# Squared-relu stages of a two-block transformer: four more output tiles as seven block products, and border squares in other buffers

## The reference, cut to what matters

```python
h2 = rms_norm_2(x, norm2) * (1.0 + scale2) + shift2
ff = jnp.square(jax.nn.relu(h2 @ w_ff1)) @ w_ff2
x = x + gate2 * ff
```

## Time and profile before

| | |
|---|---|
| runs | 3072.89, 3073.14, 3079.54 us; median 3073.14 |
| profiled execution | 3072.16 us, span 3070.4 us |
| PE busy | 3035.4 us, 99% of the span |
| DVE, ACT, POOL busy | 61%, 38%, 22% |
| granted PE clock, mean | 0.997 |
| part 3 in REL_1 | up(3, 2) to up(3, 7) 2990.54 to 3023.20 us, down(3, 0) to down(3, 7) 3023.20 to 3067 us |
| part 3 in REL_0 | 2430.94 to 2463.61 us, and 2463.61 to 2507.19 us |

### The profile page before, as it was taken

One profiled execution on the slowest core, in us unless ns is written; L12 is line 12 of the kernel. 1 busy time (PEld: TensorE's weight loads), 2 busy tenths in 40 slices (PEclk: granted clock), 3 DMA queues, 4 the chain that ended last, 5 costly groups with the idle time before them and its releaser, 6 DMA issues.

```text
span 3070.4 us, 39047 instructions
## 1 busy us (share of the span) xinstructions
PE 3035.4 (99%) x15394; PEld 2499.0 (81%) x15394; DVE 1884.7 (61%) x2899; ACT 1168.8 (38%) x1877; POOL 670.0 (22%) x525
## 2 busy tenths in 40 slices
PE   9999999999999999999999999999999999999999
PEld 7888887788888888887778888776799977779997
DVE  6454557554555445536774455677777856877775
ACT  4322334333223322234443222446544334654442
POOL 2101134111011110044311100346211123721111
PEclk9999999999999999999999999999999999999999
DMA  5343432243443434431133344310333232033232
GB/s 191 117 154 123 127 98 73 86 140 118 155 130 115 137 117 154 134 108 62 35 127 117 120 155 134 115 37 21 107 103 110 98 110 67 20 95 110 97 102 77
DMA packets 115814, 329.86 MB, mean 107 GB/s; under 512 B 13616, under 2 KB 19120, under 8 KB 115248
## 3 DMA queue, kind: packets, MB, share of 16 engines
q1 hardware_dynamic: 115632, 327.36, 33.2%
HBM read 325.21 MB, written 2.10 MB: 107 GB/s over the span
## 4 chain that ended last, share of the span: by engine, by line
PE 92%; DVE 4%; ACT 2%; POOL 1%; issue 1%; DMA 0%; SPq 0%; DVEq 0%; ACTq 0%; POOLq 0%
PE ps L83 91%; PE ps L86 1%; ACT s_tmp L89 1%; POOL s_tmp L100 1%; DVE s_wl L92 1%; DVE s_tmp L92 1%; DVE s_tmp L112 0%; DVE s_x L95 0%; ACT s_wh L89 0%; DVE s_small L106 0%; DVE s_tmp L100 0%; POOL s_tmp L92 0%; DVE s_tmpr L92 0%; ACT s_hh L89 0%; DMA s_raw<-in_f1i_dram 0%
## 5 line engine op out<-in xcount | busy, mean ns | idle before, releaser
L83 PE MATMUL ps<-s_hh,s_wh 128*128 128x512 f32 x2304 | 894.6, 393 | 20.2 <-ACT s_hh L89 11.6
L89 ACT ACTIVATE s_wh<-s_raw 128x1024 fp32r<-128x1024 f32 (+3 forms) x560 | 530.6, 951 | 951.9 <-PE ps L83 949.7
L83 PE MATMUL ps<-s_hh,s_wl 128*128 128x512 f32 x2304 | 888.2, 391 | 0.2
L83 PE MATMUL ps<-s_hl,s_wh 128*128 128x512 f32 x2304 | 887.3, 390 | 0.0
L92 DVE TENSOR_TENSOR s_wl<-s_raw,s_wh 128x1024 fp32r<-128x1024 f32 (+3 forms) x529 | 595.9, 1127 | 428.1 <-ACT s_wh L89 427.5
L92 POOL TENSOR_TENSOR s_tmp<-s_tmp 128x512 f32<-128x512 f32 (+2 forms) x228 | 306.8, 1350 | 1692.6 <-ACT s_tmp L89 1531.7
L83 PEld LDWEIGHTS ps<-s_hh,s_wh 128*128 128x128 f32 x2304 | 433.3, 188 | 117.6 <-issue 16.8
L83 PEld LDWEIGHTS ps<-s_hh,s_wl 128*128 128x128 f32 x2304 | 433.9, 188 | 93.2 <-DVE s_wl L92 2.5
L83 PEld LDWEIGHTS ps<-s_hl,s_wh 128*128 128x128 f32 x2304 | 434.1, 188 | 90.9 <-issue 2.2
L83 PE MATMUL ps<-s_a0h,s_wh 128*128 128x512 f32 (+1 forms) x1024 | 381.8, 373 | 0.0
L83 PE MATMUL ps<-s_a0h,s_wl 128*128 128x512 f32 (+1 forms) x1024 | 378.4, 370 | 0.0
(11 more groups left out here) (167 smaller groups left out, 3618.7 us busy)
## 6 DMA issues: line engine op xcount, KB each, us to landing
s_raw<-in_ff_dram SPq DMA_DIRECT2D x128, 512.0 KB, 3.7
s_tmp<-in_w_mod_dram SPq DMA_DIRECT2D x192, 256.0 KB, 3.6
s_raw<-in_f1i_dram SPq DMA_DIRECT2D x88, 512.0 KB, 3.6
s_raw<-in_f2i_dram SPq DMA_DIRECT2D x88, 512.0 KB, 3.6
s_raw<-in_f1o_dram SPq DMA_DIRECT2D x32, 512.0 KB, 3.5
s_raw<-in_f2o_dram SPq DMA_DIRECT2D x32, 512.0 KB, 3.6
s_raw<-in_hyb_dram SPq DMA_DIRECT2D x28, 512.0 KB, 3.5
s_raw<-in_nsa_dram SPq DMA_DIRECT2D x28, 512.0 KB, 3.6
```

Of the source, the lines that this page charges most:

```text
L83: return self.eng.matmul(o, w, m, **kw) if self.eng is not None else Blank()
L89: return self.eng.activation(o, a, f, **kw) if self.eng is not None else Blank()
```

## The change

In part 3 the output tiles 2 to 5 are now made by two groups, (3, 2) and (3, 4), and tiles 0, 1, 6 and 7 stay plain. So the differences, `a1h` and `a1l` are made in part 3 too, and weight sums for two more pairs. The sums are placed anew: `sum` 0 and 6 follow group(2, 6), `sum` 2 stands before group(3, 4) and `sum` 4 behind it; the buffers of PAIRS are exchanged to fit. The squares of x at the border from REL_0 to NSA_1 go to buffers 8 to 15 (which hold `hl`), as 38 to 42 are now in use by weight sums. The list of steps now ends: group(2, 6), sum 0, sum 6, up(3, 2), load, evac(3, 0), evac(3, 1), up(3, 3), load, evac(3, 2), up(3, 4), load, evac(3, 3), up(3, 5), load, evac(3, 4), up(3, 6), load, evac(3, 5), up(3, 7), load, evac(3, 6), sums, down(3, 0), evac(3, 7), load, down(3, 1), add(3, 0), load, tile 0, add(3, 1), tile 1, group(3, 2), sum 2, tile 2, tile 3, group(3, 4), sum 4, tile 4, tile 5, down(3, 6), load, down(3, 7), add(3, 6), load, tile 6, add(3, 7), tile 7.

```diff
--- before.py
+++ after.py
@@ -23,7 +23,7 @@
 FIRST_BANK = {F1_0: 4, F2_0: 0, F1_1: 4, F2_1: 0}
 GATE_BANK = (1, 0, 0, 1)
 UP_TILE = (0, 4, 1, 5, 2, 6, 3, 7)
-EARLY = (3, 2, 2)
+EARLY = (3, 2, 2, 0)
 UP_BANK = ((0, 1, 2, 3, 4, 0, 1, 2), (7, 6, 5, 0, 1, 2, 3, 4), (7, 6, 0, 1, 2, 3, 4, 5), (7, 6, 0, 1, 2, 3, 4, 5))
 LATER, SOONER = slice(T // 2, T), slice(0, T // 2)
 
@@ -467,7 +467,7 @@
     def down(p):
         for d in range(0, KT, 2):
             us = [stream.add(w2[d + m, :, p * 1024:(p + 1) * 1024], 1024) for m in range(2)]
-            if p == 3:
+            if p == 3 and d in (0, 6):
                 order.extend((("down", p, d + m), [us[m]]) for m in range(2))
             else:
                 stream.group(us)
@@ -494,9 +494,16 @@
         elif kind == "down":
             steps.append(("down", p, i, us[0]))
         else:
+            if added:
+                steps.extend([("add",) + added, ("tile", added[1])])
+                added = None
+            if p == 3 and i == 4:
+                steps.extend([("sum", 2), ("tile", 2), ("tile", 3)])
             steps.append(("group", p, i, us[0]))
             if p == 2 and i == KT - 2:
-                steps.extend([("sum", 4), ("sum", 6)])
+                steps.extend([("sum", 0), ("sum", 6)])
+            if p == 3 and i == 4:
+                steps.extend([("sum", 4), ("tile", 4), ("tile", 5)])
         if added:
             steps.append(("add",) + added)
         if kind != "group":
@@ -512,8 +519,6 @@
                 steps.append(("load", n))
             if n + 1 in stream.second and n - 1 not in stream.second:
                 steps.append(("sums", n + 1))
-            if (kind, p) == ("up", 3) and i in (3, 5):
-                steps.append(("sum", i - 3))
         if added:
             steps.append(("tile", added[1]))
             added = None
@@ -710,8 +715,8 @@
         def two(ap):
             return ap.rearrange("p (a c) -> p a c", a=2)
 
-        PAIRS = {0: (two(S(36)), two(S(37))), 2: (two(ssum2[:, :]), two(rstd[:, :])),
-                 4: (mix_tmp[:, 0:2, SOONER], mix_tmp[:, 8:10, SOONER]), 6: (mix_tmp[:, 2:4, SOONER], mix_tmp[:, 10:12, SOONER])}
+        PAIRS = {2: (two(S(36)), two(S(37))), 4: (two(ssum2[:, :]), two(rstd[:, :])),
+                 0: (mix_tmp[:, 0:2, SOONER], mix_tmp[:, 8:10, SOONER]), 6: (mix_tmp[:, 2:4, SOONER], mix_tmp[:, 10:12, SOONER])}
 
 
 
@@ -775,8 +780,8 @@
 
         parts32 = nsm[:, 0:96].rearrange("p (c j) -> p c j", j=16)
 
-        def square_slot(d):
-            return (38, 39, 40, 38, 39, 40, 41, 42)[d]
+        def square_slot(s, d):
+            return 8 + d if s == NSA_1 else (38, 39, 40, 38, 39, 40, 41, 42)[d]
 
         def square2_slot(d):
             return (43, 44, 45, 43, 44, 45, 46, 47)[d]
@@ -791,6 +796,8 @@
         gain_of = {F1_0: 0, HYB: 1, F2_0: 2, F1_1: 3, STICK: 4, F2_1: 5}
 
         def last_add(s, d, half=1):
+            if s - 1 in (REL_0, REL_1) and 2 <= d < 6:
+                return s - 1, "sum", d
             p = {F1_0: 2, HYB: 1, F2_0: 2, F1_1: 2, STICK: 1, F2_1: 2, NSA_0: 6, REL_0: 3, NSA_1: 6}[s - 1]
             return (s - 1, p, d) if half or finish_halves(s, d) == WHOLE else (s - 1, p, d, "half")
 
...
@@ -1882,8 +1889,7 @@
                         cols = LATER if p < 3 and t < 4 else slice(0, T)
                         act.wait_ge(*unit[unit_at[s, "up", p, i]])
                         if n >= 4:
-                            if n < 28:
-                                act.wait_ge(*t_dif[s, (n - 4) // 8, (n - 4) % 8 // 2, 3])
+                            act.wait_ge(*t_dif[s, (n - 4) // 8, (n - 4) % 8 // 2, 3])
                             act.wait_ge(*a_lo[s, (n - 4) // 8, UP_TILE[(n - 4) % 8]])
                         act.activation(o, B(bank_of[unit_at[s, "up", p, i]]), ACT.Relu).then_inc(*sq_up.up((s, p, i)))
                         act.wait_ge(*prod[s, p, i])
@@ -1892,7 +1898,7 @@
                         if p == 3 and i == 0:
                             act.wait_ge(*x_add[s, "sum", 7])
                         act.activation(a0h[:, t, cols], o[:, cols], ACT.Copy).then_inc(*a_hi.up((s, p, t)))
-                        if i % 2 and p < 3:
+                        if i % 2:
                             j = i // 2
                             for m in range(2):
                                 act.wait_ge(*t_dif[s, p, j, (2, 3)[m]])
@@ -2590,7 +2596,7 @@
 
 
                 r0, r1 = PAIRS[d]
-                dve.wait_ge(*x_add[s, 2, d + 1])
+                dve.wait_ge(*x_add[s, 3 if 2 <= d < 6 else 2, d + 1])
                 dve.tensor_tensor(r1[:, 0, :], r1[:, 0, :], r0[:, 1, :], ALU.add).then_inc(*x_add.up((s, d, "16")))
                 dve.wait_ge(*x_add[s, d, "16"])
                 dve.tensor_tensor(r0[:, 0, :], r0[:, 0, :], r1[:, 0, :], ALU.add).then_inc(*x_add.up((s, d, "165")))
@@ -2953,7 +2959,7 @@
                         table("gatew", gate_w, ins["nsa_gates"][l], s)
 
             def result(d):
-                sp.wait_ge(*x_add[REL_1, 3, d])
+                sp.wait_ge(*x_add[(REL_1, "sum", d) if 2 <= d < 6 else (REL_1, 3, d)])
                 sp.dma_start(out[d], x[:, d, :]).then_inc(*x_out[d].up("x", 16))
 
             def rel(s):
@@ -2966,6 +2972,9 @@
                         weights(step[3] + 4 + RING)
                     elif kind == "add" and s == REL_1:
                         result(step[2])
+                    elif kind == "sum" and s == REL_1 and step[1] in (2, 4):
+                        result(step[1])
+                        result(step[1] + 1)
 
             sp.dma_start(gains[:, :, :], ins["gains"]).then_inc(*consts["gains"].up("gains", 16))
             for d in range(KT):
```

More of the change, by code:

```diff
@@ L1167, in norm_halves @@
                 pe.wait_ge(*filled["ones"])
-                sums = [(ssum, square, square_slot, msq, 4, ssum_up, (s, KT - 3))]
+                sums = [(ssum, square, lambda d: square_slot(s, d), msq, 4, ssum_up, (s, KT - 3))]
                 if s == NSA_0:
@@ L1532, in sum_tile @@
             def sum_tile(s, d):
-                slot = square_slot(d)
+                slot = square_slot(s, d)
                 if 3 <= d < 6:
@@ L2715, in tile @@
                 if d == 0:
-                    m = pool.tensor_scalar(ssum[:, :], S(square_slot(d)), 1.0, 1.0, ALU.mult, ALU.mult)
+                    m = pool.tensor_scalar(ssum[:, :], S(square_slot(s, d)), 1.0, 1.0, ALU.mult, ALU.mult)
                 else:
                     pool.wait_ge(*ssum_up[s, d - 1])
-                    m = pool.tensor_tensor(ssum[:, :], ssum[:, :], S(square_slot(d)), ALU.add)
+                    m = pool.tensor_tensor(ssum[:, :], ssum[:, :], S(square_slot(s, d)), ALU.add)
                 m.then_inc(*ssum_up.up((s, d)))
```

## The result

The changed kernel takes 3087.89 us (median of 6 runs, 3085.88 to 3089.95) against 3074.39 us (6 runs, 3072.89 to 3079.54): ratio 1.0041, 95% interval 1.003 to 1.0052. It is slower by 13.5 us, 0.4%, and the interval leaves out 1. (The first three runs of the kernel before had a median of 3073.14 us; three more were made beside those of the changed one.) The forecast was 3084.5 us, 3077 to 3089, and slower.

The account below looks back on a forecast made before the run. PE was taken to bound the kernel (busy 3035.4 of 3070.4 us). Groups -3.2, waits at tile 7 +11.6 and clock +3.0 made +11.4 on 3072.16, 3083.6; with the median 0.98 higher, 3084.5 us, range 3077 to 3089.

Parts of the forecast that it names:

- A group saves 0.80 us: Group of 10.08 us replaces a pair of plain downs of 10.88; two groups in each of two stages: -3.2 us.
- The evacs' pace, 3.78 and 5.42 us, and 4.0 us of lag at the last: Part 3's ups: squarings 3.78 and 5.42 us apart; evacs start late and are still 4.0 us late at the last.
- +5.8 us at tile 7: down(3, 0): PE waits for tile 7's low part from 3028.19 to about 3034.0, 5.8 us a stage, +11.6 in all.
- Rivals 1 and 2: 1: evacs make good their lag, about 3073.5, chance 0.15; 2: wait at tile 7 under 1.6 us, not slower, chance 0.06.
- The sign: PE timeline, down(3, 0): one wait for `a0l` of 5 to 6 us in each stage, then granted clock under 1.
- The clock, +1.5 us a stage: After the wait at tile 7 PE's clock falls: bounds 0 and 2.5 us a stage, 1.5 taken, +3.0 in all.
- What costs nothing: Part 3's groups, later sums, tile squares, moved square buffers and weight loads were to add no time.
- rival 3: Second wait, at group(3, 2)'s second unit or the border squares: 2 to 4 us a stage more, 3089 to 3092, chance 0.07.
- The total: Sum of -3.2, +11.6 and +3.0: +11.4 us on the profiled execution's 3072.16, giving 3083.6; median forecast 3084.5.

Follow-up runs that it names:

- e3: Changed kernel, weight sums for group(3, 2) moved behind evac(3, 7), and down(3, 0) and down(3, 1) do tile 7 last: 3078.7 us.
- e8: e3 plus squares of tiles 2, 3 behind group(3, 4), sum 4 and squares of 4, 5 behind the load of down(3, 6): 3076.8 us.
- e5: Changed kernel with sums 0 and 6 behind group(2, 6) cut to four additions of one column: 3075.7 us.
- e7: Kernel before, products plain, but differences and a1h, a1l made in part 3 too, sums 0 and 2 moved behind two downs' loads: 3085.3 us.
- e1: Changed kernel with the weight sums for group(3, 2) behind evac(3, 7) instead of ahead of it: 3081.1 us.
- e9: Changed kernel, only squares of tiles 2, 3 put behind group(3, 4), sum 4 and squares of 4, 5 behind down(3, 6)'s load: 3087.4 us.
- e2: Changed kernel, but down(3, 0) and down(3, 1) run hidden tiles 0 to 6 first, then both tile 7: 3080.8 us.

## Why the prediction was right, point by point

- **A group saves 0.80 us.** Right: the groups are 10.07 and 10.08 us, and where nothing waits (REL_1 of e3 and e8) a stage is 1.63 to 1.70 us shorter. By the formula of the Trainium skill for isolated matmuls (TensorE: Matmul & The Clock Gate, back-to-back issue gap) it would be 2.4 us a stage; the runs show 1.6.
- **The evacs' pace, 3.78 and 5.42 us, and 4.0 us of lag at the last.** Right: 3.77 and 5.42. Tile 6 is squared 33.1 us behind the start of the ups, forecast 33.1 (3023.65 - 2990.54); e5 takes 4.0 us away.
- **+5.8 us at tile 7.** Right to 0.01 us in both stages, and e5's 1.83 and e7's 3.04 are the 1.8 and 3.0 that the same terms gave. Rivals 1 and 2 fell with it. The sign was named a little wrong, as one wait of 5 to 6 us for `a0l`: the rows have 3.9 us for `a0h` and 1.2 to 1.3 for `a0l`. This row-by-row sum was so good because every piece had been seen, in the same order, in another part of the same kernel. Where the order was new, in e1, the same terms gave 3.0 and the run had 1.56.
- **The clock, +1.5 us a stage.** 2.5 and 1.5, inside of 0 to 2.5. The term was mis-sized by 0.5 us a stage, and its 1.5 is met in one stage by luck: what the lower clock costs hung on how much of it fell into the wait (REL_0 none of the long piece, REL_1 some 1.7 us of it), and the sum had no such term. A lateness of 1.83 us cost none in e5, one of 3.04 us cost 1.7 in e7. The rule of the Trainium skill against idle stretches (same page, section on why this matters) would have had 2.5 us in both stages; the changed kernel's trace has it in REL_0 alone, e9's, with the same wait, in both.
- **What costs nothing.** No second wait in the changed kernel, so rival 3 fell too, but the reasoning was too easy. "ACT waits in tiles 2 and 3 for the sums, with the weight copies behind; that is wanted 15 us later" left out that DVE's own next instruction waits for that copy, and everything of DVE behind it. Sum 4 ended 6.2 us into down(3, 6) and not 4, and the square of tile 6 was in time for the norm by 0.15 us. What was called free was paid for by the wait at tile 7.
- **The total.** +11.4 us forecast in a profile, 12.4 us found in the two stretches (6.68 + 5.71). The median is 3.4 us over the forecast (3087.9 against 3084.5): 1.0 is in the stretches, 1.25 is how far the median of the kernel before rose with three more runs (3073.14 to 3074.39), and some 1.1 no trace splits. In the profiled executions the borders outside of the change cost 4.0 us more, with the granted clock at 0.50 where it was 1.00; why it falls in one execution and not in another stays open.

## What to carry to other kernels

When a saving on the bound engine is bought with work on others, look for the point at which the bound engine catches up with them, and for the last instruction ahead of it: a stretch in which an engine is half idle says nothing about a chain through three engines that starts late. Where the same chain runs elsewhere in the kernel, its rows priced the new place to a tenth of a microsecond here, as long as the order of the instructions was the same. And after taking a wait away, read the stage again: the wait had been paying for something.

## What the runs showed of the hardware

PE's clock is part of the price of a wait, and not in proportion. Waits that made a matmul 1.1 to 1.8 us late cost nothing on top (e1 in REL_1, e2 in REL_1, e5), one of 3.0 us in two pieces cost 1.7 us (e7, both stages), one of 5.8 us in two pieces cost 2.5 us and 1.5 to 1.6 in the same execution, and 2.4 to 2.5 in both stages of e9. At the border to NSA_1 waits of 3.3, 3.7 and 4.1 us (e1, e2, e3) cost 2.3, 1.1 and 2.3 us. What is lost is about half of the time that PE is busy at the lower clock, so it depends on how much of that clock falls into the wait itself. In e7 the matmuls right behind the wait still ran 0.23 us apart, and only those from 3042.15 on 0.43 (first row below). In the changed kernel the window over the end of the lower clock is the second row (length, busy times of PE, PEld, DVE, ACT, POOL, granted clock):

```profile
3042.20:3045.50 3.30, 3.30 (x9) 2.59 (x8) 3.16 (x8) 0.79 (x1) 0.00 (x0) 0.50 0.03 5
...
3044.00:3049.00 5.00, 4.32 (x12) 3.44 (x13) 4.30 (x9) 2.84 (x5) 0.00 (x0) 0.61 0.00 0
```
